# The sum of squares of a gated RMS norm: two tiles added on GpSimd before TensorE sums over partitions

## The chip, the cores and the metric

The kernel runs on one core of a Trainium2 chip, as one program. The metric is the time of one execution on the device in microseconds (us), measured over several runs; a profiled execution of the same program gives the trace that is read here. The core's engines work side by side, each from its own list of instructions: TensorE (PE in the rows; PEld is its weight load), VectorE (DVE), ScalarE (ACT), GpSimd (POOL) and SyncE (SP, which only issues DMA transfers here). They wait for each other through semaphores that the program names.

## The reference

One layer of a hybrid decoder, for 256 positions of a new sequence and 32 positions of running ones (8 sequences of 4), so 288 columns in all. After a wide input projection come a Mamba-2 SSD branch, an HGRN2 branch, a gated merge, a feed-forward part and a small gated projection. The change lies in the SSD branch, in its grouped norm:

```
y = ssd(...) + d_skip * xs                      # 4096 features = 8 groups of 512
y = (y * silu(z)).reshape(b, L, 8, 512)
y = y * rsqrt(mean(y * y, axis=-1) + 1e-6) * w  # the norm of each group by itself
```

For each column, then, the squares of 512 features of a group have to be added up. Features lie along the 128 partitions, so a group is four tiles of 128 partitions x 288 columns.

## The kernel before, in words

Everything is kept with features on partitions and the 288 columns along the free axis. Weights stream in as "slabs" of 128 x 1024 numbers in a ring of four. ScalarE copies each slab to a rounded high part (`w_hi`, L508), VectorE subtracts to get a low part (`w_lo`, L1024), and TensorE multiplies a slab as 8 x 3 matmuls of 128x288 (`multiply`, L1669 to L1671: high x high, low x high, high x low).

The SSD branch is a routine `ssd(g, first, gemm)` that every engine has in its own version. It is called for g = 0, then in a loop for g = 1 to 7, then once more for g = 8 without slabs (`gemm` false) to finish the last group. A pass of it is called pass g here. A pass has 20 steps s, one slab each on TensorE. Step by step, a pass g projects, convolves and gates the tiles of group g, and it also finishes group g - 1: its states, its output and its norm. Every engine runs its instructions in the order written; there is no planner. Around the change the order is this:

- VectorE, at step 10, multiplies the four tiles of y by silu(z) (`yf`, L1374, semaphore `sg_g`). At steps 2, 4, ..., 12 it runs a convolution: a copy (L1306), a TENSOR_SCALAR (L1308) and three SCALAR_TENSOR_TENSOR, each waiting for the one before (L1312). One step later it forms the silu of the tile (L1322, L1323).
- ScalarE, at step 10, squares `yf` into `ysq` (L745, `sg_sq`); `ysq` lies in the buffer of `xw`, which rows therefore name. At each even step from 2 to 12 it makes the tanh for the silu (L698, L699). At step 12 it waits for the sums (`sg_ms`) and takes a logarithm and an exponential (L750, L752), which give the norm's factor. At odd steps it empties the projected tiles out of PSUM (L691, L693).
- TensorE, at step 12, after that step's slab, multiplies a matrix of ones with each of the four tiles of `ysq` and accumulates (L1913); that sums over partitions and over the four tiles at once, on all partitions. Each of these float32 products is two instructions of TensorE in the trace, so a pass has eight. In pass 8 the same stands at step 11. At step 14 TensorE waits for all of the group's silus and for the logarithm (`sg_ln`), and transposes (L1941 to L1943).
- GpSimd moves data: in each pass it writes the 8 new states of the pass's running sequences to memory (L2180), and refills each of 4 buffers (`renew`, L2159) once the write has landed. After the last refill it waits for `sg_g` and loads the decays of the next group (`load_decays`, L2154 and L2156). GpSimd has no trailing call: its own `ssd(g)` writes the states and loads that go with the other engines' pass g + 1, and its last round is `ssd(7)`, outside the loop. The only arithmetic of GpSimd before is in the HGRN2 branch, a mask product `hvbd` once per head (L2122), in a loop of 15 rounds and once behind it.

Of the kernel before, what the change touches and what calls it, by code (L numbers as in the profile page):

```python
# [26 lines left out]
ALU = mybir.AluOpType  # L27
# [9 lines left out]
T = TP + TS  # L37
# [109 lines left out]
def layer_program(nc, io):  # L147
# [3 lines left out]
    def sem(name):  # L151
        return stack.enter_context(nc.semaphore(name))
# [263 lines left out]
    sg_xt, sg_xd, sg_y, sg_yf, sg_sp, sg_spe, sg_sz, sg_it, sg_su, sg_upa, sg_up = (  # L416
        sem(f"sg_{s}") for s in ("xt", "xd", "y", "yf", "sp", "spe", "sz", "it", "su", "upa", "up"))
    sg_cv, sg_ncur = sem("sg_cv"), sem("sg_ncur")
    sg_yt, sg_old = sem("sg_yt"), sem("sg_old")
    sg_xw, sg_btlo, sg_xwhi, sg_xwlo = sem("sg_xw"), sem("sg_btlo"), sem("sg_xwhi"), sem("sg_xwlo")  # L420
    sg_yi, sg_g, sg_sq, sg_ms, sg_ln, sg_rs, sg_y32 = (
        sem(f"sg_{s}") for s in ("yi", "g", "sq", "ms", "ln", "rs", "y32"))
# [1236 lines left out]
    def _(pe):  # L1659
        M = nc.tensor  # L1660
# [182 lines left out]
        def ssd(g, first, gemm):  # L1843
            r = g - 1

            def old_states(half):

                for b in range(4):
                    pe.wait_ge(sg_ht_in[b], r * 32 + 16 * (half + 1))
                pe.wait_ge(sg_cfs, g)  # L1850
                if half == 0:
                    pe.wait_ge(sg_yf, r * 4 + 3)
                for b in range(4):
                    seq = 4 * half + b
                    op = M.matmul(bank[5][TS * b:TS * b + TS, :], cfd[:, TS * seq:TS * seq + TS], ht[:, b],  # L1855
                                  start=half == 0, stop=True, skip_group_check=True)
                op.then_inc(sg_it, 1)

            def old_outputs():

                pe.wait_ge(sg_yt, g)
                for p in range(4):
                    o = T + TS * p
                    op = M.matmul(bank[4][:, o:o + TS], yt[:, P * p:P * p + P], stack4, start=True, stop=True)
                op.then_inc(sg_old, 1)

            def new_states(b):

                for i in (b, b + 1):
                    if i >= 2:  # L1870
                        pe.wait_ge(sg_up, r * NB + (i - 1))
                    M.matmul(bank[2 + i % 2][:, :], bbd[:, i], xw3[:, :], start=True, stop=True).then_inc(sg_su, 1)  # L1872

            def early_gate(u):

                t = u // 2
                if u % 2 == 0:
                    if t < 2:
                        free(T_GA + t, 0)
                    elif t == 2:  # L1880
                        pe.wait_ge(sg_yf, 4 * GROUPS)
                    else:
                        pe.wait_ge(sg_spe, GROUPS)
                multiply(*slab(U_GA, 2 * GA_SLABS, 0, u), gate_bank[t][:, 0:T], h_hi, h_lo, SK * (u % 2),
                         u % 2 == 0, u % 2 == 1)

            for s in range(SG_SLABS):
                if not gemm and s > 11:
                    break
                if gemm:  # L1890
                    t = s // 2
                    if s % 2 == 0:
                        free(T_SG + t, g * SG_TILES)
                    multiply(*slab(U_SG, SG_SLABS, g, s), ps[t % 2][:, 0:T], h_hi, h_lo, SK * (s % 2),
                             s % 2 == 0, s % 2 == 1)
                if not first:
                    if s == 0:
                        old_states(0)
                        pe.wait_ge(sg_bbd, g)
                        pe.wait_ge(sg_xwlo, g)  # L1900
                        new_states(0)
                    if s == 1:
                        new_states(2)
                    if s == 7:
                        old_states(1)
                        new_states(4)
                    if s == 8:
                        new_states(6)
                        old_outputs()
                    if s == (12 if gemm else 11):  # L1910
                        pe.wait_ge(sg_sq, g)
                        for p in range(4):
                            op = M.matmul(bank[4][:, 0:T], ones, ysq[:, p], start=p == 0, stop=p == 3)  # L1913
                        op.then_inc(sg_ms, 1)
                if not gemm:
                    if s < 4:
                        early_gate(s)
                    if s in (7, 8):
                        early_gate(s - 3)
                    if s == 11:  # L1920
                        early_gate(6)
                        early_gate(7)
                    continue
                if s == 6:

                    pe.wait_ge(sg_silu, g * XT + 2)
                    if not first:
                        pe.wait_ge(sg_spe, g)
                    M.transpose(bank[0][:, 0:P], bf[:, 0:P], ident)
                    M.transpose(bank[0][:, P:TP], bf[:, P:TP], ident)  # L1930
                    M.transpose(bank[0][0:32, TP:TP + P], bf[:, TP:T], ident)
                    M.matmul(bank[1][:, 0:TP], bf[:, 0:P], cf[:, 0:TP], start=True, stop=True)
                    M.matmul(bank[1][:, TP:TP + P], bf[:, P:TP], cf[:, P:TP], start=True, stop=True)
                    M.matmul(bank[1][0:32, 384:416], bf[:, TP:T], cf[:, TP:T], start=True,
                             stop=True).then_inc(sg_bc, 1)
                if s == 14:
                    pe.wait_ge(sg_silu, g * XT + 6)
                    if not first:
                        pe.wait_ge(sg_ln, g)
                    for c in range(4):  # L1940
                        M.transpose(bank[2][:, P * c:P * c + P], xf[:, c, 0:P], ident)  # L1941
                        M.transpose(bank[3][:, P * c:P * c + P], xf[:, c, P:TP], ident)
                        op = M.transpose(bank[4][0:32, P * c:P * c + P], xf[:, c, TP:T], ident)  # L1943
                    op.then_inc(sg_xt, 1)
                if s == 17:

                    pe.wait_ge(sg_xw, g + 1)
                    for p in range(4):
                        for b in range(2):
                            op = M.matmul(bank[1][:, P * p:P * p + P], xw[:, b, P * p:P * p + P], bt[:, b],  # L1950
                                          start=b == 0, stop=b == 1)
                    op.then_inc(sg_sp, 1)
                if s in (17, 19):
                    q = (s - 17) // 2
                    if q == 0:
                        pe.wait_ge(sg_xd, g + 1)
                        pe.wait_ge(sg_bt, g + 1)
                    else:
                        pe.wait_ge(sg_yf, g * 4 + 2)
                    pe.wait_ge(sg_m, g * 2 + (q + 1))  # L1960
                    heads = [(bank[(5, 0)[pp]], HD * hh, 4 * q + 2 * pp + hh) for pp in range(2) for hh in range(2)]
                    for y, lo, j in heads:
                        M.matmul(y[lo:lo + HD, 0:TP], xd[:, 0, HD * j:HD * j + HD], me[:, j, 0:TP],  # L1963
                                 start=True, stop=True)
                    for y, lo, j in heads:
                        M.matmul(y[lo:lo + HD, P:TP], xd[:, 1, HD * j:HD * j + HD], me[:, j, TP:TP + P],
                                 start=False, stop=True, skip_group_check=True)
                    for y, lo, j in heads:
                        op = M.matmul(y[lo:lo + HD, TP:T], xd[:, 2, HD * j:HD * j + HD],
                                      me[:, j, 384:416], start=True, stop=True)  # L1970
                    op.then_inc(sg_y, 2)
# [123 lines left out]
    def _(pool):  # L2095
# [65 lines left out]
        def ssd(g, first, last):  # L2161
# [8 lines left out]
            def renew(seq):  # L2170

                pool.wait_ge(sg_ht_out[seq % 4], g * 32 + 16 * (seq // 4 + 1))
                if seq < 4:
                    load_state(g, seq + 4)
                elif not last:
                    load_state(g + 1, seq - 4)

            for seq in range(NB):
                pool.wait_ge(sg_up, g * NB + seq + 1)
                pool.dma_start(row(io["ssm_s"], g * 2 + seq // 4)[:, seq % 4],  # L2180
                               ht[:, seq % 4]).then_inc(sg_ht_out[seq % 4], 16)
                if seq % 4:
                    renew(seq - 1)
                if seq % 4 == 3:
                    renew(seq)
            if not last:
                pool.wait_ge(sg_g, g + 1)
                load_decays(g + 1)

        pool.wait_ge(sg_raw0, 1)  # L2190
# [137 lines left out]
```

## Time and profile before

| what | value |
|---|---|
| median of three runs | 2748.74 us (2748.72 to 2751.32) |
| the profiled execution | 2750.22 us |
| its span, first to last instruction | 2748.3 us |
| TensorE busy | 2682.9 us, 98% |
| VectorE busy | 1786.0 us, 65% |
| ScalarE busy | 1421.9 us, 52% |
| GpSimd busy | 183.0 us, 7% |

The span is the time from the first to the last instruction of the program; the 1.9 us between it and the execution's time are start and end. "Busy" is the time in which at least one instruction of an engine was under way. Matmuls overlap (a 128x288 one is recorded with 0.29 us, the next starts 0.13 us later), so a busy TensorE may still have room. The SSD passes g = 1 to 7 take some 79.4 us each, from about 823 to 1374 us of the span.

### The profile page before, as it was taken

The numbers are of one execution on the slowest core, as the hardware profiler recorded it, in microseconds if no ns is written. First come the engines' busy times: TensorE is split into PE (matmuls) and PEld (weight loads), VectorE is DVE, ScalarE is ACT, GpSimd is POOL, SyncE is SP. The second block draws the span as 40 slices with busy tenths as digits, with TensorE's granted clock in tenths as the row PEclk, the third lists the DMA queues.
The fourth block names the chain that finished last, engine by engine and source line by source line (L and its number), as shares of the span: only waits on it lengthen the run. The fifth ranks groups of instructions, "written<-read, shape, count | busy, mean of one in ns | idle before, by whom it ended". The sixth has DMA issues, their size and how long they took to land.

```text
span 2748.3 us, 59421 instructions
## 1 busy us (share of the span) xinstructions
PE 2682.9 (98%) x22077; PEld 2624.0 (95%) x22077; DVE 1786.0 (65%) x3218; ACT 1421.9 (52%) x2285; POOL 183.0 (7%) x297
## 2 busy tenths in 40 slices
PE   6999999999999999999989999989999999999999
PEld 5999999999989999999989999989999999999989
DVE  7888888744478888888864444576543355554475
ACT  6667676643356655656644334454443344443363
POOL 0111111100101111111110000000000000000000
PEclk9999999999999999999999999999999999999999
DMA  4555555455556666665545556535554555555534
GB/s 171 178 170 163 178 173 168 154 189 178 180 188 215 202 208 205 204 216 197 199 166 172 179 172 206 168 120 176 166 169 162 167 161 168 168 169 167 166 131 159
DMA packets 135290, 484.22 MB, mean 176 GB/s; under 512 B 17249, under 2 KB 19697, under 8 KB 134081
## 3 DMA queue, kind: packets, MB, share of 16 engines
q1 hardware_dynamic: 114560, 410.88, 45.0%
q0 software_dynamic: 20672, 72.55, 8.3%
q8 instruction: 40, 0.66, 0.1%
q14 instruction: 18, 0.14, 0.0%
HBM read 449.58 MB, written 33.78 MB: 176 GB/s over the span
## 4 chain that ended last, share of the span: by engine, by line
PE 84%; DVE 9%; ACT 3%; issue 2%; DMA 1%; DVEq 0%; POOL 0%; ACTq 0%; POOLq 0%
PE acc L1669 25%; PE acc L1670 25%; PE acc L1671 25%; DVE w_lo L1024 2%; DVE ccv L1312 1%; ACT w_hi L508 1%; PE bank L1669 1%; PE bank L1670 1%; PE bank L1671 1%; PE bank L1855 1%; PE bank L1963 1%; PE bank L1950 1%; PE bank L1781 0%; PE bank L1872 0%; DVE x L1513 0%
## 5 line engine op out<-in xcount | busy, mean ns | idle before, releaser
L1024 DVE TENSOR_TENSOR w_lo<-raw,w_hi 128x1024 fp32r<-128x1024 f32 x772 | 936.9, 1223 | 586.9 <-ACT w_hi L508 582.7
L1669 PE MATMUL acc<-h_hi,w_hi 128*128 128x288 f32 x3872 | 1159.6, 299 | 12.4 <-DVE h_lo L1061 8.4
L1671 PE MATMUL acc<-h_hi,w_lo 128*128 128x288 f32 x3872 | 1143.1, 295 | 0.0
L1670 PE MATMUL acc<-h_lo,w_hi 128*128 128x288 f32 x3872 | 1140.8, 295 | 0.0
L508 ACT ACTIVATE w_hi<-raw 128x1024 fp32r<-128x1024 f32 x772 | 809.8, 1054 | 435.6 <-PE acc L1671 377.6
L1669 PEld LDWEIGHTS acc<-h_hi,w_hi 128*128 128x128 f32 x3872 | 728.6, 188 | 21.3 <-issue 7.4
L1670 PEld LDWEIGHTS acc<-h_lo,w_hi 128*128 128x128 f32 x3872 | 729.1, 188 | 2.8
L1671 PEld LDWEIGHTS acc<-h_hi,w_lo 128*128 128x128 f32 x3872 | 728.3, 188 | 0.0
L1669 PE MATMUL acc<-u_hi,w_hi 128*128 128x288 f32 x1024 | 303.4, 296 | 0.0
L1671 PE MATMUL acc<-u_hi,w_lo 128*128 128x288 f32 x1024 | 302.1, 295 | 0.0
L1670 PE MATMUL acc<-u_lo,w_hi 128*128 128x288 f32 x1024 | 301.4, 294 | 0.0
L1669 PEld LDWEIGHTS acc<-u_hi,w_hi 128*128 128x128 f32 x1024 | 192.5, 188 | 0.0
L1670 PEld LDWEIGHTS acc<-u_lo,w_hi 128*128 128x128 f32 x1024 | 192.5, 188 | 0.0
L1671 PEld LDWEIGHTS acc<-u_hi,w_lo 128*128 128x128 f32 x1024 | 192.4, 188 | 0.0
L1669 PE MATMUL acc<-y_hi,w_hi 128*128 128x288 f32 x384 | 113.8, 296 | 0.0
L1671 PE MATMUL acc<-y_hi,w_lo 128*128 128x288 f32 x384 | 113.3, 295 | 0.0
L1670 PE MATMUL acc<-y_lo,w_hi 128*128 128x288 f32 x384 | 113.0, 294 | 0.0
L1312 DVE SCALAR_TENSOR_TENSOR ccv<-craw,prh,ccv 128x312 f32<-128x312 f32 x144 | 78.3, 544 | 5.1
L1669 PE MATMUL acc<-m_hi,w_hi 128*128 128x288 f32 x256 | 75.8, 296 | 0.0
L1671 PE MATMUL acc<-m_hi,w_lo 128*128 128x288 f32 x256 | 75.5, 295 | 0.0
L1670 PE MATMUL acc<-m_lo,w_hi 128*128 128x288 f32 x256 | 75.4, 294 | 0.0
L1669 PEld LDWEIGHTS acc<-y_hi,w_hi 128*128 128x128 f32 x384 | 72.2, 188 | 0.0
(415 smaller groups left out, 3535.1 us busy)
## 6 DMA issues: line engine op xcount, KB each, us to landing
raw<-in_w SPq DMA_DIRECT2D x772, 512.0 KB, 3.3
ht<-in_ht POOLq DMA_DIRECT2D x64, 256.0 KB, 4.1
out_ssm_s<-ht POOLq DMA_DIRECT2D x64, 256.0 KB, 3.9
cbc<-cum_d POOLq DMA_DIRECT2D x8, 1152.0 KB, 7.0
hs<-in_s POOLq DMA_DIRECT2D x16, 512.0 KB, 4.6
out_hg_s<-hsn POOLq DMA_DIRECT2D x16, 512.0 KB, 5.0
x_in<-in_x SPq DMA_DIRECT2D x4, 576.0 KB, 5.8
mixb<-bmb POOLq DMA_DIRECT2D x16, 144.0 KB, 2.0
```

What stands on the lines that cost most here:

```text
L508: nc.scalar.activation(w_hi[:, k], raw[:, k], ACT.Copy).then_inc(hi_done, 1)
L1024: V.tensor_tensor(w_lo[:, k], raw[:, k], w_hi[:, k].bitcast(F32), ALU.subtract).then_inc(lo_done, 1)
L1312: op = V.scalar_tensor_tensor(ccv[:, 0:CVC], src[:, w:w + CVC], prh[:, c, w:w + 1], ccv[:, 0:CVC], ALU.mult, ALU.add)
L1669: M.matmul(out, w_hi[:, k, i], hi[:, kt0 + i, ::-1], start=first and i == 0, stop=False)
L1670: M.matmul(out, w_hi[:, k, i], lo[:, kt0 + i, ::-1], start=False, stop=False)
L1671: op = M.matmul(out, w_lo[:, k, i], hi[:, kt0 + i, ::-1], start=False, stop=last and i == SK - 1)
L1855: op = M.matmul(bank[5][TS * b:TS * b + TS, :], cfd[:, TS * seq:TS * seq + TS], ht[:, b], start=half == 0, stop=True, skip_group_check=True)
L1950: op = M.matmul(bank[1][:, P * p:P * p + P], xw[:, b, P * p:P * p + P], bt[:, b], start=b == 0, stop=b == 1)
L1963: M.matmul(y[lo:lo + HD, 0:TP], xd[:, 0, HD * j:HD * j + HD], me[:, j, 0:TP], start=True, stop=True)
```

## The change

GpSimd adds the second pair of tiles of squares to the first pair, in place, in one instruction; TensorE then sums two tiles in place of four. A new semaphore says that the addition is done. On GpSimd the addition stands behind the last `renew` of the pass and ahead of `load_decays`; its wait for the squares takes the place of the wait for `sg_g`. It is also done in the last round, where no decays are loaded.

```diff
-    sg_yt, sg_old = sem("sg_yt"), sem("sg_old")
+    sg_yt, sg_old, sg_sq2 = sem("sg_yt"), sem("sg_old"), sem("sg_squares_added")
...
                     if s == (12 if gemm else 11):
-                        pe.wait_ge(sg_sq, g)
-                        for p in range(4):
-                            op = M.matmul(bank[4][:, 0:T], ones, ysq[:, p], start=p == 0, stop=p == 3)
+                        pe.wait_ge(sg_sq2, g)
+                        for p in range(2):
+                            op = M.matmul(bank[4][:, 0:T], ones, ysq[:, p], start=p == 0, stop=p == 1)
                         op.then_inc(sg_ms, 1)
...
+            pool.wait_ge(sg_sq, g + 1)
+            nc.gpsimd.tensor_tensor(ysq[:, 0:2], ysq[:, 0:2], ysq[:, 2:4], ALU.add).then_inc(sg_sq2, 1)
             if not last:
-                pool.wait_ge(sg_g, g + 1)
                 load_decays(g + 1)
```

## Rows read from the trace of the kernel before

**Rows 1.** The page: the span, busy time by engine, granted TensorE clock in 40 slices.
```profile
span 2748.3 us, 59421 instructions
PE 2682.9 (98%) x22077; PEld 2624.0 (95%) x22077; DVE 1786.0 (65%) x3218; ACT 1421.9 (52%) x2285; POOL 183.0 (7%) x297
PEclk9999999999999999999999999999999999999999
```

**Rows 2.** TensorE's waits, 860 to 1352 us: us in total, times, longest.
```profile
PE bank L1941 <- DVE xf L1323: 5.2, 7, 0.8
```

**Rows 3.** TensorE's timeline, pass 3: start us, us, engine, line, operation, [idle before <-releaser].
```profile
1023.95 2.10 PE L1913 MATMUL bank<-xw,consts 128*128 128x288 f32 x8
1025.68 0.51 PE L1669 MATMUL acc<-h_hi,w_hi 128*128 128x288 f32 x1
...
1031.95 0.29 PE L1670 MATMUL acc<-h_lo,w_hi 128*128 128x288 f32 x1
1032.08 0.29 PE L1671 MATMUL acc<-h_hi,w_lo 128*128 128x288 f32 x1
1033.11 0.33 PE L1941 MATMUL bank<-consts,xf 128*128 128x128 f32 x1 [0.73 <-DVE xf L1323]
```

**Rows 4.** VectorE's timeline, pass 3.
```profile
1022.27 1.70 DVE L1312 SCALAR_TENSOR_TENSOR ccv<-craw,prh,ccv 128x312 f32<-128x312 f32 x3
...
1032.87 0.19 DVE L1323 SCALAR_TENSOR_TENSOR xf<-cth,ccv 128x32 f32<-128x32 f32 x1
```

**Rows 5.** ScalarE's timeline, pass 3.
```profile
1020.57 1.17 ACT L745 ACTIVATE xw<-yf 128x1152 f32<-128x1152 f32 x1 [3.44 <-DVE yf L1374]
1024.01 0.42 ACT L698 ACTIVATE cth<-ccv 128x256 f32<-128x256 f32 x1 [2.27 <-DVE ccv L1312]
...
1031.95 0.42 ACT L698 ACTIVATE cth<-ccv 128x256 f32<-128x256 f32 x1
```

**Rows 6.** ScalarE's waits, 954 to 1034 us.
```profile
ACT craw L691 <- PE acc L1671: 3.8, 1, 3.8
```

**Rows 7.** GpSimd's mask product L2122, and VectorE beside it and elsewhere.
```profile
L2122 POOLq MODIFY_POOL_CONFIG  x30: 11/11/11, 55.0 to 498.0; - x30
L2122 POOL TENSOR_TENSOR hvbd<-hv,consts x16: 1889/1891/1892, 69.9 to 534.5; 96x1024 fp32r<-96x1024 f32 x16
  DVE hk L1142: 208.6, 16
...
224.54 0.28 DVE L1142 TENSOR_TENSOR hk<-hkwt,hk 32x128 fp32r<-32x128 f32 x1
224.91 1.89 POOL L2122 TENSOR_TENSOR hvbd<-hv,consts 96x1024 fp32r<-96x1024 f32 x1 [12.98 <-DVE hk L1142]
...
L1146 DVE TENSOR_TENSOR hdm<-bank,consts x16: 557/558/559, 69.8 to 534.4; 128x384 f32<-128x384 f32 x16
L1413 DVE TENSOR_TENSOR cbm<-bank,consts x8: 557/557/558, 781.7 to 1335.6; 128x384 f32<-128x384 f32 x8
```

**Rows 8.** GpSimd's last state load in passes 3 and 7, TensorE's sum in pass 7.
```profile
1022.09 0.54 POOL L2159 DMA_DIRECT2D ht<-in_ht  x1 [2.32 <-DMA out_ssm_s<-ht]
...
1339.60 0.54 POOL L2159 DMA_DIRECT2D ht<-in_ht  x1 [2.13 <-DMA out_ssm_s<-ht]
1341.60 2.10 PE L1913 MATMUL bank<-xw,consts 128*128 128x288 f32 x8
```

**Rows 9.** Pass 2: GpSimd, TensorE and VectorE in their timelines.
```profile
944.52 2.10 PE L1913 MATMUL bank<-xw,consts 128*128 128x288 f32 x8
...
945.54 0.54 POOL L2159 DMA_DIRECT2D ht<-in_ht  x1 [2.05 <-DMA out_ssm_s<-ht]
...
946.13 1.23 DVE L1024 TENSOR_TENSOR w_lo<-raw,w_hi 128x1024 fp32r<-128x1024 f32 x1 [0.42 <-ACT w_hi L508]
```

**Rows 10.** Pass 8: GpSimd (the two last writes, their landing), ScalarE, TensorE, VectorE.
```profile
1403.51 1.12 POOL L2180 DMA_DIRECT2D out_ssm_s<-ht  x2 [2.30 <-DVE ht L1298]
DMA to landing us min/median/max: 2.5/2.7/2.9
...
1405.49 1.17 ACT L745 ACTIVATE xw<-yf 128x1152 f32<-128x1152 f32 x1 [7.90 <-DVE yf L1374]
1406.70 2.21 PE L1913 MATMUL bank<-xw,consts 128*128 128x288 f32 x8 [0.28 <-ACT xw L745]
1408.95 0.50 ACT L750 ACTIVATE yrs<-bank,consts 128x288 f32<-128x288 f32 x1
1426.73 0.40 PE L1669 MATMUL bank<-y_hi,w_hi 128*128 128x288 f32 x1 [1.45 <-DVE w_lo L1024]
```

**Rows 11.** TensorE's waits in the timeline; windows with the granted clock (the last but two numbers).
```profile
549.38 0.37 PE L1669 MATMUL bank<-o_hi,w_hi 128*128 128x288 f32 x1 [1.83 <-DVE w_lo L1024]
794.94 0.33 PE L1941 MATMUL bank<-consts,xf 128*128 128x128 f32 x1 [2.21 <-DVE xf L1323]
...
550.66:554.06 3.40, 3.40 (x17) 3.40 (x16) 2.40 (x3) 1.06 (x2) 0.00 (x0) 0.50 0.88 265
796.40:799.80 3.40, 3.40 (x28) 3.40 (x27) 3.08 (x6) 2.53 (x6) 0.00 (x0) 1.00 0.72 210
```

## The prediction

> **What bounds the kernel now.** I read the page first: TensorE is busy for 98% of the span at an almost always full clock [rows 1]. That invites a quick sum: the change takes 4 of the 8 TensorE instructions of L1913 out of each of eight passes, so TensorE, the busy engine, should end earlier. Whether it does is decided by the stage, so the next view was TensorE's own waits over the seven looped passes (g = 1 to 7). There is one wait and no other: before the transposes of step 14 (L1941) TensorE stands still in all seven passes, 5.2 us together, for VectorE's last silu (L1323) [rows 2]. The sum of squares belongs to step 12, 9 us ahead of that wait. So I followed one pass, the third, on each engine.
>
> TensorE starts the eight L1913 instructions at 1023.95, the next slab at 1025.68, issues its last slab matmul at 1032.08 and starts L1941 at 1033.11 [rows 3]. Slab matmuls start 0.13 us apart, so it was ready at 1032.21: 0.90 us of slack. VectorE convolves (L1312 three times, one after the other) and ends at 1023.97; ScalarE has waited 2.27 us for that, starts its tanh at 1024.01, and from there to the tanh at 1031.95 stands nowhere [rows 4, 5]. VectorE then runs the silu that ends at 1033.06 and frees TensorE [rows 4]. So from the convolution of step 10 to step 14 the bound is the chain VectorE, ScalarE, VectorE. It is tied to TensorE at the other end of a pass: in the same stretch ScalarE waits 3.8 us for a slab's last matmul before it empties the first tile (L691) [rows 6]. A pass is therefore a TensorE part (from L1941 to step 1 of the next pass), then a VectorE and ScalarE part (to L1941 again). Whatever delays L1941 lengthens the pass by as much; TensorE work taken out between step 2 and step 14 shortens nothing.
>
> **Part 1, four instructions fewer on TensorE.** The eight cover 2.10 us and one of them 0.40 [rows 3], so they start (2.10 - 0.40) / 7 = 0.243 us apart; four are 0.97 us. In the looped passes that is added to the 0.90 us that TensorE already waits: gain 0. In the eighth pass, after the loop, it counts (part 4).
>
> **Part 2, a TENSOR_TENSOR on GpSimd, 128x576.** No such instruction is in the trace. The nearest is the 96x1024 mask product of L2122, always 1.89 us [rows 7]. In proportion to the elements the add takes 576/1024 x 1.89 = 1.06 us; were all of it fixed, 1.89. I take 1.25, near the proportional end, because the work is per element, and above it because part of the 1.89 will not shrink and both operands are dense here.
>
> Is it in time? It stands behind the last load of a state in GpSimd's queue. In pass 3 that load is issued by 1022.63 and ScalarE's squares are done at 1021.74 [rows 5, 8]. A GpSimd instruction starts 0.09 us after its releaser (L1142 ends at 224.82, L2122 starts at 224.91) [rows 7]. So the add can run from 1022.72 to about 1024, where TensorE comes at 1023.95, with 0.97 + 0.90 us to spare. Passes 1 and 4 to 7 have the same phase (pass 7: 1340.14 for 1341.60 on TensorE [rows 8]). Behind the add stand the loads of the decays (L2154, L2156), some 1.4 us later than now; they are wanted by VectorE one step into the next pass, over 30 us on. Cost 0.
>
> What does it do to VectorE beside it? In pass 3 that is L1312, on the chain, whose two tensors both lie in SBUF. Below: beside L2122 VectorE's L1146 takes 558 ns, and its like L1413, with no GpSimd arithmetic beside it, 557 [rows 7]; so 0. But L1146 has one tensor in PSUM. No two-tensor SBUF instruction of VectorE runs beside L2122 in the rows: L1142 ends just ahead of it. Above: GpSimd's instruction and VectorE's exclude each other, and the chain is late by the whole add. I take the upper end, since what is undisturbed beside L2122 is another kind of instruction, and L2122 and L1312 each read two SBUF tensors. Then the add waits for the L1312 in flight (to 1022.81), runs to 1024.06, and the second L1312 starts 1.25 us late. Nothing on ScalarE absorbs it: six passes x 1.25 = 7.5 us.
>
> The Trainium skill, SBUF — State Buffer, "Who interferes with whom", says that a VectorE instruction with at most one SBUF input does not contend with GpSimd (the 558 against 557 ns agree), and that one with two contends with a GpSimd instruction that reads SBUF, by an exclusive lock held for the whole instruction. No run here yet shows the second half. By it the sum is the one below, by the rows' lower end +2.0.
>
> **Part 3, pass 2.** Here the state's write landed late and GpSimd is free only at 946.08, while TensorE comes at 944.52 [rows 9]. At 946.13 VectorE starts a w_lo (two SBUF tensors), so by the same exclusion the add waits to 947.36 and ends at 948.61. TensorE goes on at 948.7, 4.2 us late, less 0.97 and 0.90: 2.3 us. Side by side it would be 1.1.
>
> **Part 4, the eighth pass.** Here L1913 is on the path: TensorE waits for ScalarE's squares, starts at 1406.70, and its sum releases the logarithm at 1408.95 and, through VectorE's scaling and y_lo, the slab at 1426.73 that TensorE waits 1.45 us for [rows 10]. GpSimd is not free at 1406.66: it waits for the last state's landing, 2.9 us after its issue at 1404.09, so 1407.0, and some 0.2 for the wakeup. The add ends near 1408.5, TensorE starts 1.9 late and does 0.97 less: 0.9 us.
>
> Sum: 7.5 + 2.3 + 0.9 = +10.7 us. The profiled execution took 2750.2 us (its span 2748.3 and 1.9 around it) and would take 2760.9; the three timed runs have their median 1.5 lower, 2748.7, so 2759.4.
>
> **The rivals.**
> A. *Side by side*: the add slows nothing. Then only pass 2 (1.1) and the end (0.9) remain: 2750.7. For it: L1146 at 558 ns. Against: another kind of operand.
> B. *The clock.* TensorE's wait at L1941 grows from 0.74 to about 0.74 + 0.97 + 1.25 = 3.0 us. After 2.21 us of it in pass 0 the granted clock stayed at 1.00 (2.4 GHz); after 1.83 us at 549 it fell to 0.50 (1.2 GHz) for 3.4 us [rows 11]. A fall doubles the time of 1.7 us of matmuls and lies in the TensorE part of the pass. Four falls in seven: + 6.8, so 2766; seven: 2771. It adds to the forecast's mechanism only, since side by side the wait is 1.7.
> C. *Faster*: the saving counts. If TensorE's wait at L1941 is not what it seems, seven passes give 0.97 each and the end takes 0.9: -5.9, 2742.8. Against it stand seven waits out of seven.
> D. *GpSimd reloads its program.* Pool-configuration instructions stand before L2122 in its loop, 30 for 15 rounds, and none before the sixteenth, outside it [rows 7]. Should they stand before the add in the six rounds of this loop too: their price is somewhere from 0 to the 13.0 us that GpSimd idles on average ahead of L2122 (208.6 / 16), which would hide it there. At half, 6.5 us, TensorE goes on 6.5 late less 1.87 of slack: six passes make +28, with rival A's 2.0 2778. Against: L2122 itself has gone before, and the last one needed none.
> The Trainium skill, GPSIMD Engine Reference, "Instruction dispatch", gives about 6 us for the first call of freshly loaded code; no row here shows it.
>
> **How the numbers follow.** Forecast (exclusion, clock kept) 0.45, A 0.29, B 0.15, C 0.06, D 0.05. 0.2% is 5.5 us, about what can be told from no change. Forecast, B and D are slower by more, save for the case of a blocking half as long as the add (0.03): 0.62. A and that case are within: 0.32. C: 0.06. The likeliest one's own range is 2755 to 2763 (add of 1.06 to 1.6 us); to hold 8 in 10 it must take A and half of B in: 2749 to 2769.
>
> **What would show it.** The GpSimd add near 1.25 us in eight rows; the second L1312 beside it starting over 1 us late (or the three in 1.70 us still: A); L1941's waits near 3 us (A: near 1.7); in pass 8 TensorE's sum starting about 1.9 us after ScalarE's squares end; the granted clock at 1.00 after L1941. Wrong: L1941's waits unchanged (C), an add that starts several us after its inputs (D), or one that holds up only the end of the stage.

## The result, and the profile after

The changed kernel takes 2768.3 us (median of 6 runs, 2766.2 to 2770.7) against 2749.4 for the kernel before (6 runs): ratio 1.0068, 95% interval [1.0056, 1.0079], 18.9 us slower. The profiled execution took 2767.6 us, its span 2766.1 against 2748.3. The forecast was 2759.4 within 2749 to 2769: the direction and the range hold, the loss is 1.8 times the +10.7 of the sum.

The page of the kernel after, the lines of [rows 1] (before: 2682.9, 1786.0 and 183.0 us busy):

```profile
span 2766.1 us, 59365 instructions
PE 2685.8 (97%) x22045; PEld 2625.6 (95%) x22045; DVE 1798.1 (65%) x3218; ACT 1421.5 (51%) x2285; POOL 193.9 (7%) x305
PEclk9999999999999999999999999999999999999999
```

TensorE has 32 instructions fewer and more busy time, and VectorE 12 us more with as many instructions. Both are signs: matmuls ran at a lower clock somewhere, and VectorE's instructions became longer.

TensorE's waits from 870 to 1375 us in the kernel after, to set against [rows 2] (line, what it waited for, us in total, times, longest):

```profile
PE bank L1941 <- DVE xf L1323: 12.9, 6, 2.1
PE bank L1913 <- POOL xw L2187: 3.8, 3, 3.4
PE acc L1669 <- ACT craw L693: 1.9, 3, 0.6
```

The wait of step 14 grew from 0.75 to 2.15 us in every pass but the second, where there is none, and there are two new ones: for the add itself (L1913), and ahead of slab 14 (L1669) for a tile that ScalarE empties late, in passes 3, 6 and 7 and, just ahead of this window, in pass 1.

Timeline rows of the kernel after for pass 3 (the first six), pass 2 (three) and pass 8 (four), answering [rows 3 to 5], [rows 9] and [rows 10]. L2187 is the add.

```profile
1027.78 3.21 DVE L1312 SCALAR_TENSOR_TENSOR ccv<-craw,prh,ccv 128x312 f32<-128x312 f32 x3
1027.49 0.54 POOL L2159 DMA_DIRECT2D ht<-in_ht  x1 [2.16 <-DMA out_ssm_s<-ht]
1028.05 1.42 POOL L2187 TENSOR_TENSOR xw<-xw 128x576 f32<-128x576 f32 x1
1031.02 0.42 ACT L698 ACTIVATE cth<-ccv 128x256 f32<-128x256 f32 x1 [3.78 <-DVE ccv L1312]
1034.56 0.40 PE L1669 MATMUL acc<-h_hi,w_hi 128*128 128x288 f32 x1 [0.63 <-ACT craw L693]
1040.13 0.33 PE L1941 MATMUL bank<-consts,xf 128*128 128x128 f32 x1 [2.15 <-DVE xf L1323]
...
948.32 4.09 DVE L1024 TENSOR_TENSOR w_lo<-raw,w_hi 128x1024 fp32r<-128x1024 f32 x2 [0.42 <-ACT w_hi L508]
948.77 1.42 POOL L2187 TENSOR_TENSOR xw<-xw 128x576 f32<-128x576 f32 x1
950.24 1.77 PE L1913 MATMUL bank<-xw,consts 128*128 128x288 f32 x4 [3.39 <-POOL xw L2187]
...
1421.40 1.17 ACT L745 ACTIVATE xw<-yf 128x1152 f32<-128x1152 f32 x1 [6.69 <-DVE yf L1374]
1423.35 1.39 POOL L2187 TENSOR_TENSOR xw<-xw 128x576 f32<-128x576 f32 x1 [2.19 <-DMA out_ssm_s<-ht]
1423.54 2.27 DVE L1024 TENSOR_TENSOR w_lo<-raw,w_hi 128x1024 fp32r<-128x1024 f32 x1 [1.04 <-ACT w_hi L508]
1424.79 1.86 PE L1913 MATMUL bank<-xw,consts 128*128 128x288 f32 x4 [2.46 <-POOL xw L2187]
```

Three L1312 that took 1.70 us now take 3.21, and ScalarE's tanh waits 3.78 us for them instead of 2.27: 1.51 more by either count. The add beside them takes 1.42 us, here and in pass 2, where it had other work of VectorE beside it. In each of passes 3 to 7 one L1312 is stretched, from 0.54 us to 2.05, 1.76, 1.75, 1.97 and 1.98; in pass 1 the add meets L1308 instead, which takes 1.73 us.

Windows behind L1941 of the kernel after (window, span, busy time of PE, PEld, DVE, ACT, POOL with counts, granted clock, DMA share, GB/s), for [rows 11]:

```profile
1203.39:1206.80 3.41, 3.41 (x18) 3.22 (x17) 3.41 (x6) 3.41 (x8) 1.39 (x3) 0.50 0.51 129
1206.80:1210.21 3.41, 3.41 (x27) 3.41 (x27) 3.41 (x6) 0.95 (x4) 0.00 (x0) 1.00 0.74 255
1040.20:1043.61 3.41, 3.41 (x29) 3.36 (x30) 3.31 (x6) 3.41 (x9) 1.79 (x4) 1.00 0.43 91
```

Behind the wait of pass 5 TensorE ran 3.4 us at 0.50 (1.2 GHz), 18 matmuls in place of 27; behind the equal wait of pass 3 it kept 1.00 (2.4 GHz). The looped passes have five such falls, at 875.7, 950.8, 1121.5, 1203.4 and 1285.3 us; the kernel before has none in them.

Where the 17.8 us of span are, from L1941 to L1941 (79.36 to 79.50 us in every pass before):

| stretch ending at L1941 of pass | us longer | falls in it |
|---|---|---|
| 1 | 0.58 (-0.72 ahead of the squares, +1.30 behind them) | 0 |
| 2 | 4.94 | 2 |
| 3, 4 | 1.50, 1.21 | 0 |
| 5, 6, 7 | 2.80, 2.93, 3.25 | 1 each |
| the rest, to the end | 0.6 (-1.3 ahead of the squares of pass 8, +1.9 behind them) | see below |

The squares of pass 1 come 0.72 us earlier than before. The fall at 550.65 of the kernel before [rows 11], which the kernel after does not have, may be the cause; that is not shown, as L1941 of pass 0 starts anywhere from 792.9 to 794.1 us in the eight traces without a fall ahead of it. Passes 3 and 4 give the stop of VectorE: 1.36, and by their L1312 passes 5 to 7 are stopped for 1.36 in the mean as well. They are 2.99 longer, so a fall is 1.64. That leaves 4.94 - 2 x 1.64 = 1.7 for the late add of pass 2.

Pass 8 has two parts. Ahead of its squares both kernels have a fall of 6.83 us that begins in a wait of 5 us for a load: of it 6.52 us lie behind the wait in the kernel before (1394.05 to 1400.57) and 3.85 in the kernel after (1411.17 to 1415.02), so the kernel after is 1.30 shorter there. Behind the squares it is 1.9 longer, and the clock falls once more, at 1425.25, in the sum that waited for the add. By cause: stops 1.30 + 5 x 1.36 = 8.1, falls in the loop 5 x 1.64 = 8.2, pass 2 1.7, behind the last squares 1.9, less the 0.7 and the 1.3: 17.9. This is a division of one trace; the experiments test its parts.

### The profile page after: what moved, and what is told of

Its sections match the earlier page's. It is cut to its first block, busy times and chain, and to the rows that moved or that the text cites. A ratio compares the mean times of both kernels' runs of the same rounds, so it can differ in the third digit from the quotient of the medians.

```text
span 2766.1 us, 59365 instructions
## 1 busy us (share of the span) xinstructions
PE 2685.8 (97%) x22045; PEld 2625.6 (95%) x22045; DVE 1798.1 (65%) x3218; ACT 1421.5 (51%) x2285; POOL 193.9 (7%) x305
## 4 chain that ended last, share of the span: by engine, by line
PE 84%; DVE 9%; ACT 3%; issue 2%; DMA 2%; POOL 0%; DVEq 0%; ACTq 0%; POOLq 0%
PE acc L1669 25%; PE acc L1670 25%; PE acc L1671 24%; DVE w_lo L1024 2%; DVE ccv L1312 2%; ACT w_hi L508 1%; PE bank L1669 1%; DMA out_ssm_s<-ht 1%; PE bank L1670 1%; PE bank L1671 1%; PE bank L1855 1%; PE bank L1963 1%; PE bank L1950 1%; PE bank L1781 0%; DVE x L1513 0%
## 5 line engine op out<-in xcount | busy, mean ns | idle before, releaser
L1024 DVE TENSOR_TENSOR w_lo<-raw,w_hi 128x1024 fp32r<-128x1024 f32 x772 | 939.7, 1227 | 589.6 <-ACT w_hi L508 585.4
L1669 PE MATMUL acc<-h_hi,w_hi 128*128 128x288 f32 x3872 | 1163.5, 301 | 13.8 <-DVE h_lo L1061 7.1
L1669 PEld LDWEIGHTS acc<-h_hi,w_hi 128*128 128x128 f32 x3872 | 731.8, 189 | 23.9 <-issue 7.2
L1669 PE MATMUL acc<-u_hi,w_hi 128*128 128x288 f32 x1024 | 303.4, 296 | 0.0
L1669 PEld LDWEIGHTS acc<-u_hi,w_hi 128*128 128x128 f32 x1024 | 192.5, 188 | 0.0
L1669 PE MATMUL acc<-y_hi,w_hi 128*128 128x288 f32 x384 | 113.8, 296 | 0.0
L1312 DVE SCALAR_TENSOR_TENSOR ccv<-craw,prh,ccv 128x312 f32<-128x312 f32 x144 | 85.1, 591 | 5.1
L1669 PE MATMUL acc<-m_hi,w_hi 128*128 128x288 f32 x256 | 75.8, 296 | 0.0
L698 ACT ACTIVATE cth<-ccv 128x256 f32<-128x256 f32 x48 | 20.0, 417 | 106.3 <-DVE ccv L1312 106.1
```

Of the source, the lines that this page charges most:

```text
L698: nc.scalar.activation(cth[:, 0:TP], ccv[:, 0:TP], ACT.Tanh)
L1024: V.tensor_tensor(w_lo[:, k], raw[:, k], w_hi[:, k].bitcast(F32), ALU.subtract).then_inc(lo_done, 1)
L1312: op = V.scalar_tensor_tensor(ccv[:, 0:CVC], src[:, w:w + CVC], prh[:, c, w:w + 1], ccv[:, 0:CVC], ALU.mult, ALU.add)
L1669: M.matmul(out, w_hi[:, k, i], hi[:, kt0 + i, ::-1], start=first and i == 0, stop=False)
```

## The experiments

Theory: the add holds up VectorE by about its own length where VectorE is on the chain to L1941, the longer wait lets TensorE's clock fall, and TensorE's saving is worth nothing. Rivals: TensorE's saving or the order of GpSimd's queue matters; the falls come from elsewhere; any work of GpSimd stops VectorE, not its reading. All are run beside the kernel before (2749.8 to 2750.2 us).

**TensorE's half alone.** Before, with two tiles summed.

```diff
-for p in range(4):
-    op = M.matmul(bank[4][:, 0:T], ones, ysq[:, p], start=p == 0, stop=p == 3)
+for p in range(2):
+    op = M.matmul(bank[4][:, 0:T], ones, ysq[:, p], start=p == 0, stop=p == 1)
```

> The kernel before with TensorE's half of the change alone: it sums two of the four tiles of squares, and GpSimd adds nothing (half of the squares is left out). My theory: in passes 1 to 7 the chain through VectorE and ScalarE frees L1941, so the four instructions fewer (0.97 us a pass) only lengthen TensorE's wait there, from 0.74 to about 1.7 us; in pass 8 they give up to 1 us: 2748.4 us (2747 to 2750), granted clock kept. Rival, TensorE's load decides: 7 or 8 passes x 0.97 us, 2741.6 to 2742.6 us.

Measured 2749.8 us, ratio 1.000 [0.9991, 1.0009]. TensorE's waits:

```profile
PE bank L1941 <- DVE xf L1323: 12.2, 7, 1.8
```

12.2 us in seven waits against 5.2: each is longer by 1.0, the 0.97 saved. The saving turns into waiting, and waits of 1.75 us brought no fall in these passes. In pass 8, too, the saving is worth nothing: the logarithm starts 2.25 us behind the squares instead of 2.30, because ScalarE's own work ahead of it ends only then.

**The add alone.** Before, with the add into a place that nobody reads, in passes 1 to 7.

```diff
+dve.wait_ge(sg_sq2, g)                 # ahead of the next write of xd, of which spare is a part
...
-pool.wait_ge(sg_g, g + 1)
+pool.wait_ge(sg_sq, g + 1)
+nc.gpsimd.tensor_tensor(spare, ysq[:, 0:2], ysq[:, 2:4], ALU.add).then_inc(sg_sq2, 1)
```

> The kernel before with GpSimd's half alone: in passes 1 to 7 GpSimd adds the two pairs of squares into a spare tile, which only the next writer of that tile waits for; TensorE sums four tiles as before. My theory: the VectorE instruction beside the add is stretched by 1.2 to 1.5 us in six passes and the chain with it, 2757 us (2755.5 to 2760), L1941's waits near 2 us, fewer falls of the clock than the five in the changed kernel. Rival, the loss comes from TensorE's wait for the add: 2749.4 us. Rival, it is the clock alone: within 1 us of 2749.4, since TensorE has its full work.

Measured 2764.9, ratio 1.0054 [1.0041, 1.0068]: the place was right, the size too small. In the timeline of pass 3 (L1313 is L1312's line here):

```profile
1027.00 3.31 DVE L1313 SCALAR_TENSOR_TENSOR ccv<-craw,prh,ccv 128x312 f32<-128x312 f32 x3
1027.39 1.42 POOL L2191 TENSOR_TENSOR xd<-xw 128x576 f32<-128x576 f32 x1
```

The stop is 1.6 us, L1941's waits are 2.0 to 2.2 though TensorE sums four tiles, and three falls follow them, which the expected 2757 had not counted. The add by itself makes most of the loss. Pass 2 is the exception, with a wait of 0.83 only; there the add came 0.65 us into a w_lo (L1025 is L1024's line here):

```profile
950.71 1.23 DVE L1025 TENSOR_TENSOR w_lo<-raw,w_hi 128x1024 fp32r<-128x1024 f32 x1 [0.42 <-ACT w_hi L509]
951.36 1.85 POOL L2191 TENSOR_TENSOR xd<-xw 128x576 f32<-128x576 f32 x1
```

Here VectorE's instruction has its usual 1.23 us [rows 9], and the add is the one held, for 0.4 us.

**What of it stops VectorE.** The same place, with memsets, which read nothing, behind a 128x1 add that carries the wait; and with a copy, which reads one operand.

```diff
+nc.gpsimd.tensor_tensor(yrs_spare, ysq[:, 0, 0:1], ysq[:, 2, 0:1], ALU.add)
+nc.gpsimd.memset(xd[:, 0, 0:447], 0.0)      # first kernel: three memsets
+nc.gpsimd.memset(xw[:, 2, 128:512], 0.0)
+nc.gpsimd.memset(spare, 0.0).then_inc(sg_sq2, 1)
...
+nc.gpsimd.tensor_copy(spare, ysq[:, 0:2]).then_inc(sg_sq2, 1)   # second kernel
```

> The kernel before, with GpSimd work of about the add's length put beside VectorE's convolution of passes 1 to 7, which reads nothing from SBUF: a 128x1 add that carries the wait for the squares, then three memsets of 128x447, 128x384 and 128x576 floats into places that nobody reads. TensorE sums four tiles as before, and the tiles of squares are not touched, so only the company that GpSimd keeps VectorE is added. Theory 1 (what stops VectorE is GpSimd's two operand reads from SBUF): memsets don't stop it, L1312 stays at 543 ns and the time at 2750 (2748 to 2752). Theory 2 (any SBUF instruction of GpSimd stops VectorE while it runs): L1312 goes to 1.7 to 2.2 us as with the add, and the time to 2757 to 2766, 2764.9 if as with the add put aside.

> The kernel before, with a copy by GpSimd of two tiles of squares (128x2x288 floats, one operand) into a place that nobody reads, in passes 1 to 7, behind a 128x1 add that carries the wait. TensorE sums four tiles as before. Theory 1 (two operands are needed to stop VectorE): L1312 stays near 543 ns and the time at 2750 (2748 to 2752). Theory 2 (any read of SBUF stops it): L1312 grows by about the copy's own length, and the time goes to 2755 to 2766 as long as the copy takes 0.8 to 1.5 us.

Memsets: 2750.8, ratio 1.0006 [0.9996, 1.0016]. Copy: 2753.6, 1.0011 [1.0002, 1.0021]. The timelines of pass 3, memsets first:

```profile
1023.43 1.70 DVE L1314 SCALAR_TENSOR_TENSOR ccv<-craw,prh,ccv 128x312 f32<-128x312 f32 x3
1023.96 0.46 POOL L2193 MEMSET xd<- 128x447 f32 x1
1024.37 0.41 POOL L2194 MEMSET xw<- 128x384 f32 x1
```

```profile
1023.17 2.56 DVE L1314 SCALAR_TENSOR_TENSOR ccv<-craw,prh,ccv 128x312 f32<-128x312 f32 x3
1023.42 0.20 POOL L2192 TENSOR_TENSOR xd<-xw 128x1 f32<-128x1 f32 x1
1023.55 0.67 POOL L2193 COPY xd<-xw 128x576 f32<-128x576 f32 x1
```

Beside memsets the three stay at 1.70; beside the copy they gain 0.86, as long as the little add and the copy together (0.80); over the six passes that have L1314 beside the copy the gain is 0.4 to 1.0. So GpSimd's reading stops VectorE, one operand is enough, and its writing does not. By the time alone the copy is a miss (2755 expected at least): it was shorter than the 0.8 us supposed, and no fall came. The Trainium skill, SBUF — State Buffer, "Who interferes with whom", says the same of reading and writing, and this trace agrees; that the order of issue decides which engine blocks, the rows bear out only in part: VectorE was 0.25 us into its instruction here and 0.27 into it in the kernel after, and was held all the same, while 0.65 us into the w_lo of pass 2 above it was the add that was held. What decides it no run here shows.

**The add where VectorE has slack.** After, with the add behind the next pass's convolution of step 10 and TensorE's sum one step later (the add behind the refills is gone).

```diff
+if seq == NB - 1:                       # ahead of the last two refills
+    pool.wait_ge(sg_sq, g + 1)
+    if not last:
+        pool.wait_ge(sg_conv, (g + 1) * XT + 5)
+    nc.gpsimd.tensor_tensor(ysq[:, 0:2], ysq[:, 0:2], ysq[:, 2:4], ALU.add).then_inc(sg_sq2, 1)
-if s == (12 if gemm else 11):
+if s == (13 if gemm else 11):
```

> The changed kernel with the add moved: GpSimd does it ahead of the last two refills of states, and in passes 1 to 7 only when VectorE's convolution of step 10 is done; TensorE sums one step later (13). The add then falls on VectorE's silu and w_lo, behind which VectorE has 1.6 us idle. My theory: nothing on the chain is stretched, TensorE's wait at L1941 is 1.7 us as with TensorE's half alone, and the late landing of pass 2 no longer counts: 2750 us (2748.5 to 2752.5). Rival, an add on GpSimd costs its 1.4 us a pass wherever it stands: 2758 us or more. Rival, the clock falls at a wait of 1.7 us too: 2754 to 2760 us.

Measured 2750.0, ratio 1.0002 [0.9993, 1.0011]; no fall in the passes. Its timeline, pass 3:

```profile
1025.00 1.17 DVE L1322 SCALAR_TENSOR_TENSOR xf<-cth,ccv 128x256 f32<-128x256 f32 x1 [0.45 <-ACT cth L699]
1028.81 1.22 DVE L1024 TENSOR_TENSOR w_lo<-raw,w_hi 128x1024 fp32r<-128x1024 f32 x1 [1.40 <-ACT w_hi L508]
...
1024.48 1.41 POOL L2186 TENSOR_TENSOR xw<-xw 128x576 f32<-128x576 f32 x1 [6.21 <-DVE ccv L1312]
```

The add still stops VectorE (L1322 takes 1.17, 0.43 without it), but VectorE waits 1.40 us for ScalarE soon after, so nothing comes later. With the whole change in and the cost hidden, the time is that of before.

**The add ahead of the refills** instead of behind them, waiting for the squares alone (it stands behind the issue of the last write, not ahead of it as the expectation says).

```diff
+if seq == NB - 1:
+    pool.wait_ge(sg_sq, g + 1)
+    nc.gpsimd.tensor_tensor(ysq[:, 0:2], ysq[:, 0:2], ysq[:, 2:4], ALU.add).then_inc(sg_sq2, 1)
```

> The kernel after, with the add ahead of GpSimd's last write of a state block and the refills behind it, instead of behind them; the add itself waits for the squares alone, as before. Theory 1 (the lost time has three parts: the add that stops VectorE in passes 3 to 7, the add that comes late in passes 2 and 8 behind the refills, and the falls of TensorE's clock behind L1941): the wait of L1913 in passes 2 and 8 shrinks, pass 2 costs 1.5 to 2 like passes 3 and 4 instead of 5, and the time is 2763 to 2766, from 2768.3. Rival (the late add costs nothing, pass 2 loses its time by the clock alone): 2767 to 2769.

Measured 2766.3, ratio 1.006 [1.0043, 1.0077], within the range but by another sum. Pass 2 costs 2.69 instead of 4.94 and no L1913 waits in a looped pass; but now every pass from 2 to 7 takes 82.1 to 82.3, as each has a fall. In pass 3:

```profile
1026.90 1.61 DVE L1308 TENSOR_SCALAR ccv<-craw,prh 128x312 f32<-128x312 f32 x1
...
1026.92 1.40 POOL L2184 TENSOR_TENSOR xw<-xw 128x576 f32<-128x576 f32 x1 [3.97 <-ACT xw L745]
```

The add now meets L1308, which reads one tensor, and that goes from 0.44 to 1.61.

**Eight instructions again on TensorE**, to fill its wait (after, the two tiles summed twice).

```diff
-for p in range(2):
+for p in (0, 1, 0, 1):
```

> The changed kernel, with TensorE summing the two tiles twice over (the second time from the start again), so that it has eight instructions again. If TensorE's longer standstill before L1941 (2.1 us, with 0.6 more a slab ahead) is what lets the clock fall, it shrinks by 0.97 us and the falls mostly go: 2768.3 less four or five falls of 1.65 us, 2761 us (2759.5 to 2764). If the falls have another cause: 2768 us. If TensorE's load decides: 2768.3 + 7 x 0.97 = 2775 us.

Measured 2770.8, ratio 1.0075 [1.0061, 1.0089]: the theory's time did not come. Five of L1941's waits are 2.06 to 2.13 us still (one is 1.48), and behind each of the five the clock falls. In the kernel after, TensorE had waited 0.63 us ahead of slab 14 in pass 3; here no such wait is left, so the added work took its place first and shortened L1941's wait by only 0.1. So the wait was not filled; the next kernel fills it.

**Filling the wait itself.** After, with 14 useless matmuls ahead of the wait of L1941.

```diff
+if not first:
+    for _ in range(14):
+        M.matmul(bank[2][:, 0:T], h_hi[:, 0, 0:P], h_hi[:, 0, ::-1], start=True, stop=True)
```

> The kernel after, with 14 matmuls without use on TensorE in front of its wait at L1941, in passes 2 to 8, into a bank that is free there, so that TensorE isn't idle in the wait. The add, its place and the wait for the conversion are those of the kernel after. Theory 1 (the falls of the granted clock behind L1941 come from TensorE's idle time there, and cost 1.65 us each): no stretch at 0.50 is left between 870 and 1375 us, the periods of passes 5 to 7 come down from 82.2 to 82.6 to those of passes 3 and 4 (80.6 to 80.9), and the time is 2760 (2757 to 2763). Rival (the falls have another cause, or the fillers delay slab 14): the falls stay, 2767 to 2770, or later by the fillers' length.

Measured 2763.5, ratio 1.0051 [1.0034, 1.0067]: 4.8 us less than the kernel after, and half a microsecond above the range expected. TensorE's timeline at L1941 of pass 5, and two windows behind such waits:

```profile
1199.58 2.02 PE L1939 MATMUL bank<-h_hi 128*128 128x288 f32 x14
1201.90 0.33 PE L1944 MATMUL bank<-consts,xf 128*128 128x128 f32 x1 [0.29 <-DVE xf L1323]
```

```profile
1201.90:1205.30 3.40, 3.40 (x28) 3.35 (x29) 3.25 (x7) 3.40 (x9) 1.85 (x4) 1.00 0.43 91
1283.00:1286.40 3.40, 3.40 (x29) 3.35 (x28) 3.40 (x6) 3.40 (x9) 1.65 (x4) 1.00 0.46 118
```

(The expectation counts the passes of the fillers from 1; they are passes 1 to 7 here.) L1941 still waits for VectorE, and yet the falls behind it are gone: passes 3 to 7 all take 80.8 to 81.0 us. Two falls are left up to the end of the loop, both at waits without fillers: at 948.0, in the wait for pass 2's late add, and at 794.4, behind L1941 of pass 0. The mean granted clock bears it out beyond the one trace: 0.996 to 0.997 in all four executions, 0.991 to 0.994 in the six of the kernel after. So the falls do come from TensorE's idle time, and with them away the stop is worth 1.5 a pass, and a fall 2.99 - 1.5 = 1.5. Four falls fewer would be 6 us or more, and the time shows 4.8; the fall at 794.4, which the trace of the kernel after does not have, may account for the rest.

**A shorter chain.** Before, with VectorE's state updates of blocks 6 and 7 moved from step 9 to step 12 and no add; then the change with the same updates moved and the add behind the same convolution as in the kernel that hid it (in GpSimd's list it stands ahead of the last two writes there).

```diff
-if s in (1, 2, 8, 9):
-    update({1: 0, 2: 2, 8: 4, 9: 6}[s])
+if s in (1, 2, 8, 12 if gemm else 9):
+    update({1: 0, 2: 2, 8: 4, 12 if gemm else 9: 6}[s])
...
+    pe.wait_ge(sg_up, g * NB)           # at step 14, ahead of L1941
```

> The kernel before, with VectorE's last pair of state updates (blocks 6 and 7) moved from step 9 to step 12 of passes 2 to 7, behind the conversion that L1941 waits for; no add. If the chain of VectorE and ScalarE up to that conversion ends each pass, the conversion comes earlier by the updates' length, and what is left is TensorE's idle time there, 1.7 us a pass, of which some 0.9 can go: six or seven passes, 2743.5 (2740 to 2746). Rival (the updates are late for the state's write and the next pass, or another wait takes the place): 2749 to 2755.

> The change with its add placed where VectorE has slack (behind the last convolution of the next pass, TensorE's sum one step later), and the updates of blocks 6 and 7 moved behind the conversion as in the kernel beside it. If the chain is shorter than TensorE's own work in the pass, TensorE's saving of 0.97 us a pass begins to count: 2741 (2738 to 2744), below the kernel with the updates moved alone. Rival (the chain still ends the pass, so the saving is worth nothing here too): the same as that kernel, or slower where the add now meets another VectorE instruction of the chain, 2744 to 2752.

The updates alone: 2745.1, ratio 0.9983 [0.9974, 0.9992], faster than both kernels; a pass takes 78.80. (The expectation puts the updates behind the last conversion, and in passes 2 to 7; they stand ahead of that conversion, in passes 1 to 7, and fill 1.64 us that VectorE used to wait for ScalarE there.) With the add: 2748.1, 0.9991 [0.9982, 1.0]; a pass takes 79.03, and the expected gain of TensorE's saving is not there. The waits of TensorE in the two:

```profile
PE bank L1942 <- DVE xf L1323: 1.1, 6, 0.2
```

```profile
PE bank L1942 <- DVE xf L1323: 9.9, 7, 1.6
```

**Is the saving worth anything there?** The kernel with the updates moved, two tiles and no add; and the one with add and updates, with the add halved.

```diff
-for p in range(4):
-    op = M.matmul(bank[4][:, 0:T], ones, ysq[:, p], start=p == 0, stop=p == 3)
+for p in range(2):
+    op = M.matmul(bank[4][:, 0:T], ones, ysq[:, p], start=p == 0, stop=p == 1)
...
-nc.gpsimd.tensor_tensor(ysq[:, 0:2], ysq[:, 0:2], ysq[:, 2:4], ALU.add)
+nc.gpsimd.tensor_tensor(ysq[:, 0], ysq[:, 0], ysq[:, 1], ALU.add)   # TensorE: tiles 0, 2, 3
```

> The kernel with the updates moved alone (2745.1 us, a period of 78.80 us in which TensorE waits only 0.16 at L1941), and TensorE sums two tiles instead of four; no add, so half of the squares is left out. Theory 1 (in that kernel TensorE ends the pass and the chain has some 0.5 us to spare: the kernel with add and updates moved has a period of 79.03, of which the add's stretch of L1322 is 0.75, so the chain alone takes 78.28): the period falls to 78.3, L1941 waits again, and the time to 2741.5 (2740 to 2743). Rival (the chain ends the pass at 78.8 too): 2744 to 2746, TensorE's saving worth nothing here as in the kernel before.

> The kernel with add and updates moved, with half of the add: GpSimd adds one tile of squares to another (288 columns instead of 576), and TensorE sums three tiles instead of four or two. Theory 1 (a stop of VectorE is as long as GpSimd's instruction beside it, less what VectorE was idle anyway): the add takes some 0.8 us, from 0.1 us after the last L1312's release, against 0.45 us in which VectorE waits for ScalarE, so L1322 is stretched by 0.2 to 0.3 us instead of 0.75, the period is 78.5, and the time 2743 (2741.5 to 2744.5). Rival (the stretch is the same whatever the length): the period stays at 79.0 and the time at 2746 to 2748.

Two tiles, no add: 2745.2, 0.9985 [0.9976, 0.9994]. Half the add: 2745.6, 0.9985 [0.9976, 0.9994]. Both take 78.80 a pass, as the updates alone do: the rival held in the first, and neither theory gave 78.8 for the second. My subtraction (79.03 less the 0.75 by which the add stretched L1322) was wrong, since part of a stretch is hidden. The half add's timeline, pass 3:

```profile
1021.71 0.56 DVE L1322 SCALAR_TENSOR_TENSOR xf<-cth,ccv 128x256 f32<-128x256 f32 x1 [0.45 <-ACT cth L699]
1022.66 1.23 DVE L1024 TENSOR_TENSOR w_lo<-raw,w_hi 128x1024 fp32r<-128x1024 f32 x1 [0.29 <-ACT w_hi L508]
...
1021.19 0.80 POOL L2184 TENSOR_TENSOR xw<-xw 128x288 f32<-128x288 f32 x1 [8.61 <-DVE ccv L1312]
```

L1322's 0.13 us more come out of the wait behind it (0.29, 0.42 with no add). Why the saving still buys nothing is in the chain of waits of the kernel with two tiles (start, us, what):

```profile
1083.20 1.00 PE bank L1855 x8
1084.19 0.44 PE bank L1872
1084.68 0.69 issue
1085.37 0.77 DVE ht L1294 x2
...
1109.50 0.22 ACT cth L699
1109.92 0.16 issue
1110.09 0.20 DVE xf L1323
1110.41 0.32 PE bank L1942
```

The pass is TensorE's up to the products of the new states, and VectorE's and ScalarE's from there to L1941's line. L1913 lies beside the second half. No saving there counts, with the chain as long as before or as short as it was made here.

## Why the prediction came out as it did

- *What bounds the kernel, and Part 1 (saving worth 0)*: right. Two tiles alone changed nothing, neither in the kernel before (1.000) nor in the one with a shorter chain (2745.2 us for 2745.1).
- *Part 2, price and place of the add*: 1.42 us measured for an estimate of 1.25 between 1.06 and 1.89; it started at once behind the last load, as worked out. That the decays behind it cost nothing is borne out by the kernel that hid the add, which has them later too.
- *Part 2, exclusion*: right, and the upper end was the one to take. It was forecast at 1.25 in six passes, 7.5 together, and is 8.1 (1.30 in pass 1, 1.36 after). But I let the add wait for the instruction in flight, and forecast the second L1312 late; instead the instruction in flight is stretched (L1312 in passes 3, 6 and 7, L1308 in pass 1, a w_lo in pass 2). In passes 4 and 5 the add starts 0.01 to 0.02 us ahead of L1312.
- *Part 3*: 2.3 forecast, about 1.7 by difference, in a pass with two falls; the split is not shown more closely than by moving the add ahead of the refills (pass 2: 2.25 shorter, with one fall less).
- *Part 4*: 0.9 forecast, 1.8 measured from the squares to the logarithm (4.13 us for 2.30), 1.9 to the end of the span; that the table's 0.6 comes near the forecast is luck. The add starts 0.8 us behind the squares (1423.35, 1422.56; 0.5 worked out), and TensorE waits 2.46 us instead of 0.28, so its sum starts 2.2 later for a forecast of 1.9. Then the clock falls in the sum: its four instructions take 1.86 us, and 1.24 at the full clock in the kernel with the add ahead of the refills.
- *L1941's wait*: 3.0 forecast, 2.15 measured; in passes 1, 3, 6 and 7 some 0.63 of the rest came ahead of slab 14.
- *The step that failed is "clock kept"*. I made rival B (0.15) a case beside the forecast because one wait of 2.21 us had kept the clock [rows 11]. That was one trace: the same wait of 2.2 us, at L1941 of pass 0, stands in all fourteen traces of this document, ahead of every change, and in ten of them the clock fell at it. The falls came on top of the forecast, five in the loop, 8.2 us by the trace; filling the wait took the four at L1941 away and 4.8 us. The time, 2768, is that of B between its four falls (2766) and seven (2771); that it lies within the forecast's range is owed to the half of B that the range took in.
- *Rivals A, C and D* are refuted: by the stretched L1312, by the two tiles alone, and by an add that starts within 0.1 us of the load ahead of it in passes 1 to 7, with no pool-configuration instruction before it.

What stays open: why equal waits of some 2.1 us sometimes keep the clock. The kernel after lost it behind four of six of them, the add ahead of the refills behind six of seven, the eight instructions behind five of five, the add alone behind three of six.

The wait of pass 0 shows both outcomes most plainly. In the kernel before it kept the clock [rows 11]; in the kernel that hid the add, with the same instructions up to there, it did not (a timeline row, and a window read as above):

```profile
793.61 0.40 PE L1941 MATMUL bank<-consts,xf 128*128 128x128 f32 x1 [2.22 <-DVE xf L1323]
793.74:797.15 3.41, 3.41 (x17) 3.16 (x18) 2.86 (x3) 3.41 (x9) 1.28 (x3) 0.50 0.62 156
```

## What to carry to other kernels

An engine at 98% is no reason to take work from it: look for the wait that ends last in that stage, and try the saving alone. GpSimd arithmetic on SBUF tensors is not free work on an idle engine; where it reads SBUF it can hold up VectorE for about its length, as it did in most passes here, so put it where VectorE waits for someone soon after. When a change makes TensorE wait longer at one place in a loop, count the matmuls behind that wait at half the clock as part of the forecast, not as a rival, and do not take one wait that kept the clock in one trace as a sign that the next will.

## What had not been expected of the hardware

- A VectorE instruction already running can be stretched by a GpSimd one that starts after it: 0.54 to 2.05 us beside an add of 1.42. It is not always so: beside a w_lo 0.65 us under way the add took 1.85 and the w_lo its usual 1.23.
- L1308, a TENSOR_SCALAR that reads one tensor, is held as well (0.44 to 1.61 us), though L1146, which reads one tensor from SBUF and one from PSUM, is not [rows 7]. Reading one tensor from SBUF is not by itself a shelter, as the prediction's words on it suggest. The Trainium skill, SBUF — State Buffer, "Who interferes with whom", excepts tensor_scalar where it runs in a mode that takes both ports; the row agrees with that, without showing the mode.
- GpSimd memsets beside VectorE cost it nothing: three L1312 in 1.70 us with and without.
